# Compression weights as the moving operand: 32 stationary token columns in four column tiles, sums folded and turned by an identity

## What is computed

```
def compress_blocks(tok, pos, w1, b1, w2, n_cmp):
    bsz = tok.shape[0]
    idx = CMP_STRIDE * jnp.arange(n_cmp)[:, None] + jnp.arange(CMP_BLOCK)[None, :]
    blk = tok[:, idx] + pos[:, None, :]
    blk = blk.transpose(0, 1, 3, 2, 4).reshape(bsz, n_cmp, NSA_KV_GROUPS, CMP_BLOCK * NSA_HEAD_DIM)
    return jax.nn.gelu(blk @ w1 + b1) @ w2
...
    k_cmp = compress_blocks(kv[:, :, 0], cmp_pos_k, cmp_w1_k, cmp_b1_k, cmp_w2_k, n_cmp)
    v_cmp = compress_blocks(kv[:, :, 1], cmp_pos_v, cmp_w1_v, cmp_b1_v, cmp_w2_v, n_cmp)
```

## Time and profile before

| | us |
|---|---|
| runs of the kernel | 3070.22, 3081.81, 3073.18 |
| median | 3073.18 |
| the profiled execution, its own time | 3075.42 |
| its span in the profile | 3073.7 |
| PE busy | 3028.3 |
| DVE busy | 1851.5 |
| ACT busy | 1479.2 |
| mean granted clock of PE | 0.995 |

### The profile page before, as it was taken

How to read it: one execution, slowest core, us unless ns; L and a number is a source line. 1 busy time by engine, 2 the same in 40 slices (tenths; PEclk the granted TensorE clock), 3 DMA queues, 4 the chain that set the end, 5 groups by cost and what they waited for, 6 DMA issues and landing times.

```text
span 3073.7 us, 38949 instructions
## 1 busy us (share of the span) xinstructions
PE 3028.3 (99%) x15839; PEld 2579.6 (84%) x15839; DVE 1851.5 (60%) x2319; ACT 1479.2 (48%) x2159; POOL 80.3 (3%) x153
## 2 busy tenths in 40 slices
PE   8999999999999999999999999999999999999999
PEld 6889888888888889788888988898888889888887
DVE  5556655547655546754555665568775546877554
ACT  5445544435544435643544554444655434465542
POOL 0000000000000001100000000100000000000000
PEclk9999999999999999999999999999999999999999
DMA  6563555555555555255556355564154557524453
GB/s 227 191 212 125 171 192 185 187 184 190 196 181 192 185 191 186 99 182 191 185 192 212 124 172 191 192 199 153 69 178 151 180 190 200 168 81 165 151 180 135
DMA packets 293348, 533.00 MB, mean 173 GB/s; under 512 B 27650, under 2 KB 116148, under 8 KB 293172
## 3 DMA queue, kind: packets, MB, share of 16 engines
q1 hardware_dynamic: 279908, 511.63, 51.0%
q10 hardware_dynamic: 13264, 18.90, 1.8%
HBM read 528.33 MB, written 1.11 MB: 172 GB/s over the span
## 4 chain that ended last, share of the span: by engine, by line
PE 94%; DVE 2%; ACT 2%; DMA 1%; issue 1%; POOL 0%; ACTq 0%; SPq 0%; POOLq 0%; DVEq 0%
PE bank L715 91%; PE bank L1001 2%; PE bank L1029 1%; ACT sb_hT_high L1266 1%; DMA sb_ring<-in_w_xq_dram 1%; DVE sb_sc L1964 0%; ACT sb_parts L1292 0%; PE bank L775 0%; PE bank L767 0%; DVE sb_parts L1783 0%; DMA sb_o_rows<-in_mem_dram 0%; ACT sb_sc L1428 0%; DVE sb_prT L1974 0%; DMA sb_ring<-in_ff_w_in_dram 0%; PE bank L792 0%
## 5 line engine op out<-in xcount | busy, mean ns | idle before, releaser
L1783 DVE TENSOR_TENSOR sb_parts<-sb_ring,sb_parts 128x2048 fp32r<-128x2048 f32 x480 | 1098.3, 2292 | 804.6 <-ACT sb_parts L1292 802.6
L715 PE MATMUL bank<-sb_parts,sb_hT_high 128*128 128x512 f32 (+1 forms) x4608 | 1392.2, 389 | 8.4 <-DVE sb_parts L1783 5.2
L1292 ACT ACTIVATE sb_parts<-sb_ring 128x2048 fp32r<-128x2048 f32 x480 | 914.9, 1913 | 802.5 <-PE bank L715 690.4
L715 PEld LDWEIGHTS bank<-sb_parts,sb_hT_high 128*128 128x128 f32 x4608 | 857.3, 190 | 185.6 <-issue 11.6
L715 PE MATMUL bank<-sb_parts,sb_hT_low 128*128 128x512 f32 (+2 forms) x2304 | 870.1, 387 | 0.0
L715 PE MATMUL bank<-sb_parts,sb_hidden_high 128*128 128x512 f32 x1760 | 545.9, 391 | 0.0
L715 PEld LDWEIGHTS bank<-sb_parts,sb_hT_low 128*128 128x128 f32 x2304 | 436.1, 189 | 88.4
L715 PEld LDWEIGHTS bank<-sb_parts,sb_hidden_high 128*128 128x128 f32 x1760 | 329.7, 188 | 73.1 <-issue 0.6
L715 PE MATMUL bank<-sb_parts,sb_hidden_low 128*128 128x512 f32 x880 | 345.5, 393 | 0.0
L715 PE MATMUL bank<-sb_hT_high,sb_parts 128*128 128x256 f32 x1408 | 255.0, 283 | 0.0
L715 PEld LDWEIGHTS bank<-sb_hT_high,sb_parts 128*128 128x128 f32 x1408 | 220.2, 192 | 0.2
(11 more groups left out here) (215 smaller groups left out, 2130.0 us busy)
## 6 DMA issues: line engine op xcount, KB each, us to landing
sb_ring<-in_ff_w_in_dram SPq DMA_DIRECT2D x160, 1024.0 KB, 5.2
sb_ring<-in_ff_w_out_dram SPq DMA_DIRECT2D x88, 1024.0 KB, 4.9
sb_ring<-in_w_in_dram SPq DMA_DIRECT2D x42, 1024.0 KB, 5.2
sb_ring<-in_w_gate_up_dram SPq DMA_DIRECT2D x40, 1024.0 KB, 5.2
sb_ring<-in_a_w_qkv_dram SPq DMA_DIRECT2D x24, 1024.0 KB, 5.1
sb_ring<-in_w_down_dram SPq DMA_DIRECT2D x22, 1024.0 KB, 5.0
sb_ring<-in_ff_w_in_dram SPq DMA_DIRECT2D x32, 512.0 KB, 4.9
sb_ring<-in_c_w_qkv_dram SPq DMA_DIRECT2D x12, 1024.0 KB, 5.1
```

Of the source, the lines that this page charges most:

```text
L715: return nc.tensor.matmul(o, lhsT, rhs, start=start, stop=stop)
L1292: nc.scalar.activation(halves(n, slice(0, filled(n))).high, ring[:, raw_in[n], 0:filled(n)], ACT.Copy) \
L1783: V.tensor_tensor(both.low, ring[:, raw_in[n], 0:filled(n)], both.high.bitcast(F32), ALU.subtract) \
```

## The change

Stationary and moving operand of the compression products change places. `blk` is padded from 15 to 16 blocks a group, so that its 30 token columns become 32 (a `memset` writes zeros into the two padding columns), and is the stationary operand; the moving operand is a depth step's whole 256 columns of weights. Of the 8 depth steps in a chunk, steps j and j + 4 write to the same 32 partitions of one bank, and four neighbouring steps write to the four different groups of 32 partitions (the column tiles of the array). After both chunks the bank holds four partial sums, with tokens in partitions. ACT copies it into `tmp` (`hid_sums`), and two matmuls with a constant matrix `fold`, an identity repeated four times, add the four sums and turn the result so that hidden columns are in partitions again. The Gelu then reads that. `fold` is built once, at the start, by one DVE reduction of the identity.

```
-        blk = flat[:, 4 * S:4 * S + 960].rearrange("p (v j g c) -> p v j g c", v=2, j=16, g=2)
+        blk = flat[:, 4 * S:8 * S].rearrange("p (v j g c) -> p v j g c", v=2, j=16, g=2)
...
                     def compress(h):
                         arrived((*L, "cmp", v, h))
                         wv = raw_view((*L, "cmp", v, h))
+                        for j in range(8):
+                            r = 32 * (j % 4)
+                            ins = mm(hid_bank[r:r + 32, 0:CMP_HIDDEN], blk[:, v, 8 * h + j, :, :].rearrange("p g c -> p (g c)"),
+                                     wv[:, j, :], h == 0 and j < 4, h == 1 and j >= 4)
+                        key = (st, "hid sums", v) if h else (st, "hid half", v)
+                        ins.then_inc(matmul_done.sem, matmul_done.next(key))
+                        chunk_end[(*L, "cmp", v, h)] = key
+
+                    rows_gemm([(*L, "merge", c, h) for h in range(2)], (st, "merge", c), hT, banks, compress if banks else None)
+                    if banks:
+                        hid_bank = YB.take(pe, (st, "hid", v))
+                        pe.wait_ge(dve_step.sem, dve_step.at("fold"))
+                        pe.wait_ge(act_read.sem, act_read.at((st, "hid sums", v)))
                         for f in range(2):
-                            for j in range(8):
-                                ins = mm(hid_banks[f][:, 0:30], wv[:, j, f * P:(f + 1) * P],
-                                         blk[:, v, 8 * h + j, :, :].rearrange("p g c -> p (g c)"), h == 0 and j == 0, h == 1 and j == 7)
...
+                            ins = mm(hid_bank[:, f * 2 * N_CMP:(f + 1) * 2 * N_CMP], hid_sums[:, v, f * P:(f + 1) * P],
+                                     fold[:, :, 0:N_CMP], True, True)
+                        ins.then_inc(matmul_done.sem, matmul_done.next((st, "hid", v)))
...
+                step(V.memset(blk[:, :, :, :, N_CMP:CMP_STRIDE].rearrange("p v j g c -> p (v j g) c"), 0.0))
...
+                step(V.tensor_reduce(fold[:, :, :], ident[:, :].rearrange("p (n g c) -> p g c n", n=4, g=2), AX.X, ALU.add), "fold")
```

More of the change, by code:

```diff
@@ L276, in build @@
         ident = sb("ident", [P, P])
+        fold = sb("fold", [P, 2, CMP_STRIDE])
         minus_half = sb("minus_half", [P, 16])
@@ L386, in build @@
         tok2 = flat[:, 0:4 * S].rearrange("p (v g s) -> p v g s", v=2, g=2)
-        blk = flat[:, 4 * S:4 * S + 960].rearrange("p (v j g c) -> p v j g c", v=2, j=16, g=2)
+        blk = flat[:, 4 * S:8 * S].rearrange("p (v j g c) -> p v j g c", v=2, j=16, g=2)
+        hid_sums = tmp[:, :].rearrange("p (v n) -> p v n", v=2)
         psum = [ctx.enter_context(nc.psum_tensor(f"bank{i}", [P, 512], F32)) for i in range(8)]
@@ L1113, in branches @@
                         pe.wait_ge(dve_read.sem, dve_read.at((st, "blk", v)))
-                        hid_banks = [YB.take(pe, (st, "hid", v, f)) for f in range(2)]
+                        hid_bank = YB.take(pe, (st, "hid sums", v))
                         banks = [G.take(pe, ((st, "merge", c), t)) for t in range(NT)]
@@ L1119, in compress @@
                         wv = raw_view((*L, "cmp", v, h))
-                        for f in range(2):
-                            for j in range(8):
-                                ins = mm(hid_banks[f][:, 0:30], wv[:, j, f * P:(f + 1) * P],
-                                         blk[:, v, 8 * h + j, :, :].rearrange("p g c -> p (g c)"), h == 0 and j == 0, h == 1 and j == 7)
-                            key = (st, "hid", v, f) if h else (st, "hid half", v, f)
-                            ins.then_inc(matmul_done.sem, matmul_done.next(key))
+                        for j in range(8):
[4 more added lines that the diff above has]
+                        ins.then_inc(matmul_done.sem, matmul_done.next(key))
                         chunk_end[(*L, "cmp", v, h)] = key
                     rows_gemm([(*L, "merge", c, h) for h in range(2)], (st, "merge", c), hT, banks, compress if banks else None)
+                    if banks:
+                        hid_bank = YB.take(pe, (st, "hid", v))
+                        pe.wait_ge(dve_step.sem, dve_step.at("fold"))
+                        pe.wait_ge(act_read.sem, act_read.at((st, "hid sums", v)))
+                        for f in range(2):
+                            ins = mm(hid_bank[:, f * 2 * N_CMP:(f + 1) * 2 * N_CMP], hid_sums[:, v, f * P:(f + 1) * P],
+                                     fold[:, :, 0:N_CMP], True, True)
+                        ins.then_inc(matmul_done.sem, matmul_done.next((st, "hid", v)))
                     if c == 3:
                         pe.wait_ge(small_loaded.sem, small_loaded.at(st))
-                        pe.wait_ge(act_read.sem, act_read.at((st, "hid", 1, 1)))
+                        pe.wait_ge(act_read.sem, act_read.at((st, "hid", 1)))
                         product((st, "kc"), [(w2k[:, f, :, :].rearrange("p u d -> p (u d)"), hid_c[:, 0, f, :]) for f in range(2)], 30,
@@ L1558, in branches @@
                         v = c - 1
[L1559 to L1563, removed]
+                        act.wait_ge(matmul_done.sem, matmul_done.at((st, "hid sums", v)))
+                        copy(hid_sums[:, v, :], G.of((st, "hid sums", v))[:, 0:CMP_HIDDEN]) \
+                            .then_inc(act_read.sem, act_read.next((st, "hid sums", v)))
                     for t in range(NT):
@@ L1567, in branches @@
                             .then_inc(act_read.sem, act_read.next(((st, "merge", c), t)))
+                    if c in (1, 2):
+                        act.wait_ge(matmul_done.sem, matmul_done.at((st, "hid", v)))
+                        for f in range(2):
+                            ins = nc.scalar.activation(hid_c[:, v, f, :], G.of((st, "hid", v))[:, f * 2 * N_CMP:(f + 1) * 2 * N_CMP],
+                                                       ACT.Gelu_apprx_tanh, bias=gcol((("cmp_b1_k_2", "cmp_b1_v_2")[v], l), f))
+                        ins.then_inc(act_read.sem, act_read.next((st, "hid", v)))
                     if c == 4:
@@ L2260, in branches @@
                             pos = gT[:, t_, r + 8 * half:r + 8 * half + 8].unsqueeze(2).broadcast_to([P, 8, N_CMP])
-                            ins = V.tensor_tensor(blk[:, v, 8 * half:8 * half + 8, g, :], src, pos, ALU.add)
+                            ins = V.tensor_tensor(blk[:, v, 8 * half:8 * half + 8, g, 0:N_CMP], src, pos, ALU.add)
                     ins.then_inc(dve_read.sem, dve_read.next((st, "blk", v)))
```

## The result

| | us |
|---|---|
| kernel before, median of 16 runs | 3074.4 |
| changed kernel, median of 16 runs | 3080.9 (3078.3 to 3085.5) |
| ratio | 1.0019, 95% interval 1.0012 to 1.0026 |
| span of the profiled execution after | 3081.1 (before 3073.7) |

The forecast was 3058, the range 3054 to 3066. The kernel became 6 us slower instead of 15 us faster. That is inside half a per cent of no change, but the forecast missed by 23 us, and two large terms hide behind the small difference.

What follows compares the result with a forecast made beforehand. PE was taken to bound the kernel, with DVE next: PE alone would free 27.8 us, but DVE's low halves cap this at 9.4 + 5.7 = 15.1. So 3073.2 - 15.1 = 3058 us, range 3054 to 3066.

Steps and rivals of the forecast that it cites:

- What bounds the kernel: Whole kernel: PE, busy 99% of the span with 94% of the chain; DVE full and slightly ahead from `blk` on.
- The block, X: Compression block on PE: 16 new records would take 0.9 to 1.9 us, against 3.8 before.
- Serial tiles: Rival for the compression blocks: column tiles do not overlap, 3.7 us a block, kernel at 3063.6; chance 0.16.
- The fold: On PE behind merge 1.1 and merge 2.1: two instructions of four records in all, 0.5 us.
- What is late next, up to `kc`: C1 to `kc`: PE waits for DVE's low halves, capping savings at 9.4 and 5.7 us, 15.1 in all.
- What is late next, behind `kc`: After the compression stretch: PE is behind DVE again from merge 3.0, and the later chain shifts along, keeping 15.1 us.
- The price of `fold`: At the start: the one-time reduction for `fold` costs nothing on the path, or 0.3 us if not hidden.
- the likeliest class: Whole kernel: "same", within half a per cent (15.4 us) of no change; chance 0.68.
- The clock: C1 to `kc` on PE: granted clock restored to 1.00, since the new records are dense or few.
- 10.6 left over: C1 to `kc` before: 6.9 and 3.7 us beyond merge and compression, put down to PE's half clock.
- the rival: Clock still falls behind blocks, 1.7 us each, mostly absorbed by PE's waits behind C1 to C3; about 3062.5; chance 0.10.
- ACT's copy: Before PE's fold: ACT's copy of the sums causes 0 wait, at most 0.5 us in layer 1; late-copy rival 0.07.

Runs made afterwards that it cites:

- e8_one_tile: e1_fold_last with all 16 matmuls of the sums writing to the same 32 partitions, so no column tiles run side by side; 3066.7 us, ratio to before 0.9974.
- e1_fold_last: The changed kernel with `fold` allocated behind the arena, so every other tile starts where it did before; 3069.4 us, ratio to before 0.9981.
- e7_copies_early: e1_fold_last with DVE copying `kc` and `vc` out one chunk earlier, behind the low half of merge 5.0; 3062.2 us, ratio to before 0.9957.
- e12_half_taps: e7_copies_early with one convolution tap instead of two ahead of each merge-stretch chunk, result incomplete; 3050.1 us, ratio to before 0.9913.

## Why the prediction was wrong, point by point

- *What bounds the kernel.* Right: PE by its share, DVE close behind from `blk` on. DVE's rows of the changed kernel have no gap there, and the periods are the same as in the earlier trace rows:

```profile
2092.53 2.29 DVE L1797 TENSOR_TENSOR sb_parts<-sb_ring,sb_parts 128x2048 fp32r<-128x2048 f32 x1
2094.74 6.42 DVE L2227 SCALAR_TENSOR_TENSOR sb_arena<-sb_arena,sb_convwT 128x256 f32<-128x256 f32 x16
2101.07 2.29 DVE L1797 TENSOR_TENSOR sb_parts<-sb_ring,sb_parts 128x2048 fp32r<-128x2048 f32 x1
```

- *The block, X.* Right: 1.07 us, between 0.92 and 1.84. *Serial tiles* was worked out as 48.7 us from C1 to `kc` and a gain of 9.6 us; e8_one_tile, which has serial tiles, takes 49.1 us there and gains 8.4, and its block of 3.64 us is the 3.68 of the sum. The rule of the Trainium skill ("TensorE: Matmul & The Clock Gate", "Part 3: Packing small matmuls") that weight loads overlap matmuls only in other row groups would make the block serial; the trace does not agree, at 1.07 against 3.64 us. Its figure for three column tiles, 2.38 times, gave an estimate of 1.2 to 1.6 us; four tiles measured 3.4 times.
- *The fold.* Right: 0.52 us against 0.5.
- *What is late next, up to `kc`.* Right: 15.7 us against 15.1, and in e1_fold_last `kc` begins at 2110.36, where the sum had put it at 2110.4. With the wait for the instruction ahead of it the memset delayed `blk` by 0.6 us in layer 0 and by 0.25 in layer 1 rather than by 0.17.
- *What is late next, behind `kc`.* This step failed. The text had PE behind DVE again from merge 3.0 on and all that follows shift along; it followed the low halves alone. The banks of `latT` were not followed to their reader: DVE's copy of `kc` stood behind the low half of merge 5.1, 6.6 us ahead of PE in layer 0 and 2.9 us in layer 1. A gain of 9.3 and 6.4 us is more than that slack, so 2.96 and 2.92 us came back as a wait, in layer 1 with a stretch of half clock behind it. e7_copies_early gives 7 us back.
- *The price of `fold`.* This step failed, and it is the one that turned the sign. The forecast put "the one-time reduction for `fold`" among what costs nothing on the path, and had no term for the tile itself. The reduction does cost nothing. The 128 bytes of the tile, in front of the arena, cost 11.4 us in code that the change does not touch. No term of the sum and no rival had a place outside the stage. That the result still lies in the likeliest class, within half a per cent of no change, is luck: 15.7 us gained and 23.1 us lost happen to be near each other.
- *The clock.* It stayed at 1.00 behind C4 in both layers, and the one stretch at half clock that was left, behind C1 of layer 0, PE's waits absorbed, as the rival said. What the clock had cost before was underrated: 15% of 55.1 us and 10% of 51.9 are 8.3 and 5.2 us, 13.5 in all, where the sum had 10.6 left over. That the clock falls behind other new idle time of PE was not put at all.
- *ACT's copy.* No wait in the changed kernel; visible in e12_half_taps, where the cover is gone.

## What to carry to other kernels

A new tile is part of a change's cost: look at what is allocated behind it, and where the hot matmuls get slower with it, move them back by putting the new tile last, or try paddings; here the best distance between the stationary and the moving operand was 0 modulo 256 bytes. When PE gets faster ahead of a slower engine, follow every operand and every bank that PE takes afterwards to the engine that frees or writes it and write down the slack; what is gained beyond the smallest comes back as a wait. And check a forecast first at the start of the changed stage: if the two profiles differ there already, the cause lies outside.

## What the runs showed of the hardware that I had not expected

A 128x512 one-pass matmul costs 226.8 ns or up to 233.3 ns by how far apart its two operands start in SBUF (table above). Over 2640 matmuls that is 17 us of this kernel, and the kernel before with 64 and with 128 unused bytes measured 3068.7 and 3086.6 us. With four column tiles of 32 a block took 1.07 us against 3.64 with one, whether neighbouring instructions go to different tiles (1.07 us) or two by two to the same (1.09 us). By the starts of the records, four begin within 0.02 us and the next four 0.22 us behind them, where one tile begins a single record every 0.22 us: four times the rate. The block's 3.4 times come from the last records, which take 0.4 us in both. Changing to these narrow tiles was not free: the first record of a block starts 0.32 us after the last 128x512 record, and the old block's started after 0.23.
